# A trunk kernel on one core: weight rows spread by TensorE instead of by DMA, and three of eight channel blocks convolved by TensorE instead of two

## What is computed

```python
def rms_norm(x, g):
    xf = x.astype(jnp.float32)
    y = xf * lax.rsqrt(jnp.mean(xf * xf, axis=-1, keepdims=True) + NORM_EPS)
    return (y * g.astype(jnp.float32)).astype(x.dtype)
...
def conformer_conv(hn, w_in, b_in, w_dw, b_dw, ln_g, ln_b, w_out, b_out):
    a = hn @ w_in + b_in
    u, gate = jnp.split(a, 2, axis=-1)
    u = u * jax.nn.sigmoid(gate)
    u = lax.conv_general_dilated(u, w_dw[:, None, :], window_strides=(1,),
                                 padding=((CONV_WIDTH - 1, 0),),
                                 dimension_numbers=('NWC', 'WIO', 'NWC'),
                                 feature_group_count=D_MODEL) + b_dw
    u = jax.nn.silu(layer_norm(u, ln_g, ln_b))
    return u @ w_out + b_out
...
        q = (xc @ w_q).reshape(PEER_TOKEN_CHUNK, PEER_HEADS, 2, PEER_D_HALF)
        s = jnp.einsum('thcd,hcnd->thcn', q, subkeys, preferred_element_type=jnp.float32)
        s_top, i_top = lax.top_k(s, PEER_TOPK)
        cand = s_top[:, :, 0, :, None] + s_top[:, :, 1, None, :]
        cand_idx = i_top[:, :, 0, :, None] * PEER_N_KEYS + i_top[:, :, 1, None, :]
        best, pos = lax.top_k(cand.reshape(PEER_TOKEN_CHUNK, PEER_HEADS, PEER_TOPK * PEER_TOPK), PEER_TOPK)
        idx = jnp.take_along_axis(cand_idx.reshape(PEER_TOKEN_CHUNK, PEER_HEADS, PEER_TOPK * PEER_TOPK), pos, axis=-1)
        g = jax.nn.softmax(best, axis=-1)
        u = u_tab[idx]
        act = jax.nn.gelu(jnp.einsum('td,thkd->thk', xc, u), approximate=False)
        v = v_tab[idx]
        return jnp.einsum('thk,thkd->td', (g * act).astype(v_tab.dtype), v)
...
        h = h + mix
        h = h + peer_ffn(rms_norm(h, norm_ffn[layer]), peer_w_q[layer], peer_subkeys[layer],
                         peer_u[layer], peer_v[layer])
    return rms_norm(h, norm_final)
```

## Time and profile before

| | |
|---|---|
| median of 3 runs | 1570.3 us (1569.29 to 1572.05) |
| profiled execution, its own time | 1571.79 us |
| its span in the profile | 1570.0 us |
| busy: TensorE, its weight loads | 1026.8 us (65%), 505.7 us (32%) |
| busy: VectorE | 1100.7 us (70%) |
| busy: ScalarE, GpSimd | 597.5 us (38%), 602.9 us (38%) |
| moved by DMA | 613.86 MB, 391 GB/s over the span |
| mean granted clock of TensorE | 0.733 of 2.4 GHz |

### The profile page before, as it was taken

How to read it: one execution, slowest core, us unless ns; L and a number is a source line. 1 busy time by engine, 2 the same in 40 slices (tenths; PEclk the granted TensorE clock), 3 DMA queues, 4 the chain that set the end, 5 groups by cost and what they waited for, 6 DMA issues and landing times.

```text
span 1570.0 us, 20460 instructions
## 1 busy us (share of the span) xinstructions
PE 1026.8 (65%) x6572; PEld 505.7 (32%) x6572; DVE 1100.7 (70%) x2959; ACT 597.5 (38%) x1794; POOL 602.9 (38%) x516
## 2 busy tenths in 40 slices
PE   7988766667467677766676677467677645544443
PEld 3545422323234345322244355123234301101000
DVE  3433877776445679999665679699876676666764
ACT  2222455452143434444343434344434523332321
POOL 0002444443323345644334356244434444433441
PEclk9999996577777688667889799556688855555555
DMA  9627999999999999999999999999999999999996
GB/s 393 215 74 305 379 418 420 412 419 393 418 398 415 417 418 404 393 419 392 419 415 415 417 416 408 420 416 402 409 397 391 418 419 418 420 419 419 420 419 258
DMA packets 96156, 613.86 MB, mean 391 GB/s; under 512 B 11057, under 2 KB 16433, under 8 KB 27441
## 3 DMA queue, kind: packets, MB, share of 16 engines
q0 software_dynamic: 73728, 536.90, 83.3%
q1 hardware_dynamic: 21600, 75.47, 12.3%
q10 hardware_dynamic: 720, 0.18, 0.1%
HBM read 611.46 MB, written 1.05 MB: 390 GB/s over the span
## 4 chain that ended last, share of the span: by engine, by line
DMA 34%; DVE 27%; PE 19%; issue 12%; ACT 6%; POOL 2%; DVEq 0%; SPq 0%; POOLq 0%; ACTq 0%
DMA ring<-table_dram,idx 28%; DVE ring L1614 11%; PE bank L587 8%; PE ypsum L587 4%; DVE arena L1499 4%; PE qpsum L587 4%; DMA head<-heads_dram 3%; PE spsum L587 2%; POOL ring L580 2%; ACT L1030 2%; DMA arena<-c_out_dram 1%; ACT ring L1030 1%; DVE topi L1548 1%; ACT wts L1030 1%; PE bank L592 1%
## 5 line engine op out<-in xcount | busy, mean ns | idle before, releaser
L580 POOL DMA_INDIRECT ring<-table_dram,idx x512 | 602.7, 1177 | 942.3 <-PE ypsum L587 674.3
L1614 DVE CUSTOM_DVE_ANT_0 ring<-xns,ring 128x1024 f32<-128x1024 f32 x512 | 622.7, 1222 | 306.2 <-DMA ring<-table_dram,idx 303.1
L587 PE MATMUL ypsum<-ring,wts 128*32 128x256 f32 x4096 | 427.4, 512 | 453.8 <-ACT wts L1030 451.5
L1030 ACT ACTIVATE gel<-dot 128x1 f32<-128x1 f32 x512 | 103.3, 202 | 770.5 <-DVE dot L1614 769.1
L587 PEld LDWEIGHTS ypsum<-ring,wts 128*32 128x32 f32 x4096 | 100.1, 126 | 703.5 <-ACT wts L1030 654.4
L1030 ACT ACTIVATE wts<-gident,gel 128x32 f32<-128x32 f32 x512 | 164.6, 321 | 17.0 <-ACT gel L1030 0.2
L587 PE MATMUL qpsum<-head,hT 128*128 128x256 f32 (+1 forms) x308 | 92.8, 462 | 28.1 <-DMA head<-heads_dram 24.2
L1030 ACT ACT_TABLE_LOAD x84 | 107.8, 1283 | 8.5 <-PE bank L592 7.0
L1499 DVE SCALAR_TENSOR_TENSOR arena<-arena,cols 128x128 f32<-128x128 f32 x360 | 103.9, 344 | 0.7
L587 PEld LDWEIGHTS qpsum<-head,hT 128*128 128x128 f32 (+1 forms) x308 | 68.4, 230 | 50.9 <-issue 21.9
L587 PE MATMUL bank<-hT,arena 128*128 128x128 f32 x512 | 76.9, 312 | 2.8 <-issue 2.8
(11 more groups left out here) (162 smaller groups left out, 1045.5 us busy)
## 6 DMA issues: line engine op xcount, KB each, us to landing
head<-heads_dram SPq DMA_DIRECT2D x28, 512.0 KB, 9.2
ring<-w_in_dram SPq DMA_DIRECT2D x4, 2048.0 KB, 17.1
ring<-table_dram,idx POOLq DMA_INDIRECT x512, 12.6
arena<-c_in_dram SPq DMA_DIRECT2D x4, 2048.0 KB, 15.4
arena<-heads_dram SPq DMA_DIRECT2D x7, 1152.0 KB, 25.2
arena<-heads_dram SPq DMA_DIRECT2D x26, 256.0 KB, 5.1
arena<-c_out_dram SPq DMA_DIRECT2D x6, 1024.0 KB, 10.8
arena<-w_out_dram SPq DMA_DIRECT2D x1, 4096.0 KB, 38.5
```

What stands on the lines that cost most here:

```text
L580: pool.indirect_dma_start(out=row(b), out_offset=None, in_=table[:, :], in_offset=bass.IndirectOffsetOnAxis(ap=idx[R % 2][:, k:k + 1], axi ...
L587: return nc.tensor.matmul(o_, l, r, start=start, stop=stop, **kw)
L1030: return nc.scalar.activation(out_, in_, func, **kw)
L1614: V.tensor_tensor_reduce(out=u, in0=xnr[G % 2], in1=u, scale=1.0, scalar=0.0, op0=ALU.mult, op1=ALU.add, accum_out=dot[:, k:k + 1]).then_i ...
```

## The change

1. The norm weights of phases 1 to 3 and of the final norm, and the convolution's bias, are loaded as one row into partition 0 only. TensorE spreads the row over 128 partitions: a product of a row of ones (`ones`, 1x128) with the row (1x512) for each half. For a norm this takes two bank jobs more (`N_ROW`), filled by `gains` one slot before VectorE's norm (slot 93 or 94; slot 80 of the last phase), and VectorE reads the weights out of the banks in two instructions of 128x512 instead of one of 128x1024. For the bias the product is added to `conv_out`'s bank, and VectorE's addition of the bias and the wait behind it go. Phase 0's weights still come in the old way.
2. Block 5's taps go from VectorE to TensorE and ScalarE: TensorE makes blocks 6, 7 and 5, VectorE first 0, 1, 2, then 3 and 4. The slots over which they are spread stay. In VectorE's second part each tap waits for all but the last instruction instead of all but the last two.
3. Two small tiles move into the space of another (`posi`, `posf`), and the final norm signals each half.

```diff
-N_PROJ, N_NORM = 2 + len(PROJ_CHUNKS), 2
+N_PROJ, N_NORM = 2 + len(PROJ_CHUNKS), 4
+N_ROW = 2
...
-GLU_ORDER = [0, 1, 2, 6, 7, 3, 4, 5]
+GLU_ORDER = [0, 1, 2, 6, 7, 5, 3, 4]
...
-DVE_TAPS = [(c, k) for three in ((0, 1, 2), (3, 4, 5)) for k in range(TAPS) for c in three]
-PE_TAPS = [(c, k) for c in (6, 7) for k in range(TAPS)]
+DVE_TAPS = [(c, k) for some in ((0, 1, 2), (3, 4)) for k in range(TAPS) for c in some]
+PE_TAPS = [(c, k) for c in (6, 7, 5) for k in range(TAPS)]
...
             def load_gain(p):
                 n = min(p // TILES, LAYERS)
-                sp.dma_start(xn, gains_in[n:n + 1, :].to_broadcast([P, D])).then_inc(gain_in, 16)
+                if p == 0:
+                    sp.dma_start(xn, gains_in[n:n + 1, :].to_broadcast([P, D])).then_inc(gain_in, 16)
+                else:
+                    sp.dma_start(xn[0:1, :], gains_in[n:n + 1, :]).then_inc(gain_in, 16)
...
-                sp.dma_start(cbias, c_bout[0:1, :].to_broadcast([P, D])).then_inc(cbias_in, 16)
+                sp.dma_start(cbias[0:1, :], c_bout[0:1, :]).then_inc(cbias_in, 16)
...
-                last = gemm(CONV_AT[t] + J_CW + i, [hT_[:, k, :] for k in range(KD)], [cout[:, k, :] for k in range(KD)], CHUNK, half)
+                j, n = CONV_AT[t] + J_CW + i, out_half(t, i) * CHUNK
+                bank = bank_of(pe, j) if half == 0 else banks[bank_no(j)]
+                for k in range(half * KD // 2, (half + 1) * KD // 2):
+                    last = mm(bank[:, :], hT_[:, k, :], cout[:, k, :], k == 0, False)
                 if half == 0:
                     last.then_inc(cout_taken, 1)
+                else:
+                    pe.wait_ge(cbias_in, 16 * (t + 1))
+                    mm(bank[:, :], ones[0:1, :], cbias[0:1, n:n + CHUNK], False, True).then_inc(bank_full[bank_no(j)], 1)
...
+            def gains(p):
+
+                pe.wait_ge(gain_in, 16 * (p + 1))
+                for half in range(2):
+                    j = NORM_AT[p] + half
+                    bank = bank_of(pe, j)
+                    mm(bank[:, :], ones[0:1, :], xn[0:1, half * CHUNK:(half + 1) * CHUNK], True, True).then_inc(bank_full[bank_no(j)], 1)
...
+                if s == NORM_SLOT[p - 1] - 1:
+                    gains(p)
                 if s == NORM_SLOT[p - 1] + 1:
                     turn_input(p)
...
-                dve.wait_ge(cbias_in, 16 * (t + 1))
-                V.tensor_tensor(xs, xs, cbias[:, n:n + CHUNK], ALU.add).then_inc(half_done, 1)
-                dve.wait_ge(half_done, 2 * t + i + 1)
...
-                dve.wait_ge(gain_in, 16 * (p + 1))
-                V.scalar_tensor_tensor(out=xn, in0=xt(p % TILES), scalar=r, in1=xn, op0=ALU.mult, op1=ALU.mult)\
-                 .then_inc(xn_ready, 1)
+                for half in range(2 if p else 0):
+                    j, at_ = NORM_AT[p] + half, slice(half * CHUNK, (half + 1) * CHUNK)
+                    full(dve, j)
+                    free(j, V.scalar_tensor_tensor(out=xn[:, at_], in0=xt(p % TILES)[:, at_], scalar=r, in1=banks[bank_no(j)][:, :],
+                                                   op0=ALU.mult, op1=ALU.mult))
```

More of the change, by code:

```diff
@@ L85 @@
 NORM_AT += [CONV_AT[0] + N_CONV, CONV_AT[1] + N_CONV]
+NORM_AT.append(NORM_AT[PHASES - 1] + N_NORM)
 BANKS = 3
@@ L302, in build @@
         smalli = sb("smalli", 2, i32)
-        posi = sb("posi", TILES, i32)
-        posf = sb("posf", TILES)
+        posi, posf = sel[:, 0:TILES].bitcast(i32), sel[:, TILES:2 * TILES]
         rnorm = sb("rnorm", TILES)
         warm = sb("warm", 1)
+        ones = sb("ones", P)
         rows, rinv = part["sums"][:, 0:ATTN_HEADS], part["sums"][:, ATTN_HEADS:2 * ATTN_HEADS]
@@ L853, in beside_conv @@
                     conv_out(t, 1, s - 90)
-            def turn_input(p):
-                pe.wait_ge(xn_ready, p + 1)
-                turn_over(NORM_AT[p], xn)
+            def gains(p):
[4 more added lines that the diff above has]
+                    mm(bank[:, :], ones[0:1, :], xn[0:1, half * CHUNK:(half + 1) * CHUNK], True, True).then_inc(bank_full[bank_no(j)], 1)
+            def turn_input(p):
+                if p == 0:
+                    pe.wait_ge(xn_ready, 1)
+                else:
+                    for half in range(2):
+                        emptied(pe, NORM_AT[p] + half)
+                turn_over(NORM_AT[p] + N_ROW, xn)
             def replicate(G):
@@ L889, in head_queries @@
                 if p and h == 0:
-                    emptied(pe, NORM_AT[p])
-                    emptied(pe, NORM_AT[p] + 1)
+                    emptied(pe, NORM_AT[p] + 2)
+                    emptied(pe, NORM_AT[p] + 3)
                 bank = bank_of(pe, q_job(H))
@@ L995, in _ @@
             turn_input(0)
-            emptied(pe, NORM_AT[0])
-            emptied(pe, NORM_AT[0] + 1)
+            pe.wait_ge(ones_ready, 1)
+            emptied(pe, NORM_AT[0] + 2)
+            emptied(pe, NORM_AT[0] + 3)
             early_heads()
@@ L1023, in _ @@
                     beside_heads(p + 1, s)
+                elif s == FINAL_SLOT - 2:
+                    gains(PHASES)
         @block.scalar
@@ L1137, in take_taps @@
                 full(act, j)
-                for i in range(2):
+                for i in range(len(PE_TAPS) // TAPS):
                     c = PE_TAPS[i * TAPS][0]
@@ L1206, in turn_input @@
                 for i in range(2):
-                    take(NORM_AT[p] + i, xnT[:, 4 * i:4 * i + 4, :].rearrange("p k t -> p (k t)"))
+                    take(NORM_AT[p] + 2 + i, xnT[:, 4 * i:4 * i + 4, :].rearrange("p k t -> p (k t)"))
             def replicate(G):
@@ L1497, in tap @@
                     return
-                own.wait(2)
+                own.wait(2 if c < 3 else 1)
                 own.did(V.scalar_tensor_tensor(
@@ L1666, in final @@
                 r = rms(xt(t), D)
-                dve.wait_ge(gain_in, 16 * (PHASES + 1))
-                V.scalar_tensor_tensor(out=xt(t), in0=xt(t), scalar=r, in1=xn, op0=ALU.mult, op1=ALU.mult)\
-                 .then_inc(final_ready, 1)
+                for half in range(2):
+                    j, xs = NORM_AT[PHASES] + half, xt(t)[:, half * CHUNK:(half + 1) * CHUNK]
+                    full(dve, j)
+                    V.scalar_tensor_tensor(out=xs, in0=xs, scalar=r, in1=banks[bank_no(j)][:, :], op0=ALU.mult, op1=ALU.mult)\
+                     .then_inc(final_ready, 1)
             project(0)
             project(1)
+            V.memset(ones[:, :], 1.0).then_inc(ones_ready, 1)
             dve.wait_ge(ident_in, 2 * 16)
```

13 lines of the change are left out of this document (8 added, 5 removed).

## The result

The changed kernel took 1560.2 us (median of 6 runs, 1558.1 to 1562.6) against 1569.8 for the kernel before in the same session: a ratio of 0.9944, 95% interval 0.9932 to 0.9956, which is 8.8 us less (6.9 to 10.7); the two medians by themselves are 9.6 apart. That is inside the range, 3 us above the forecast. The profiled execution took 1561.3 us, its span 1559.4, 10.6 less than the one before; this is a difference of two single executions, and the ratio is the firmer number.

The account below looks back on a forecast made before the run. The prediction took DMA transfers at 419 GB/s as the bound. From a median of 1570.3 us, loads -7.5, taps -7.0 and ends +0.6, +0.5, +0.2 summed to -13.2, giving 1557.1 us, with a range of 1551 to 1566.

Parts of the forecast that it names:

- What bounds it: Whole kernel: DMA transfers are the limit, at a full rate of 419 GB/s; no gather slot can average under 2.50 us.
- The six loads: Four norm and two bias loads shrink from 128 rows to one, each saving 1.25 us at full rate: -7.5 us.
- the low bound: Four of the six loads lie in tap stretches where DMA is short of work; if worthless, only 2.5 us remain.
- The taps: In both tap stretches, 31 taps a convolution leave VectorE, regaining seven tenths of 9.9 us lost: -7.0 us, bounds 0 and 9.9.
- 412 GB/s or more: Sign of success: DMA's rate in the two tap stretches, before at 402 and 410 GB/s, reaches at least this.
- ScalarE and TensorE: In the tap stretches they take 31 more taps, 10.5 us on ScalarE and 13.3 on TensorE each, covered on average.
- 0.43 us a tap: TensorE's cost in the tap stretches for one more tap, at 1.2 GHz; 31 make 13.3 us.
- The ends: Convolution ends +0.6 us, later weights +0.5, final norm and the rest +0.2, where the row spreading adds work.
- the quarter counted for the weights' second half: Second output product's later weights, asked for 0.92 us later: a quarter counted, +0.5 us in all, bounds 0 and 1.8.
- A: Rival: only the bytes pay; TensorE's and ScalarE's lateness in the tap stretches replaces VectorE's; 1564.1 us, chance 0.18.
- B: Rival: not measurably faster; the taps bring nothing and loads inside the tap stretches only filled idle time; 1569.1 us, chance 0.07.
- C: Rival: slower, TensorE becomes the bound while taps run if its clock falls to about 1.2 GHz; 1580.6 us, chance 0.07.

Follow-up runs that it names:

- wide loads: The changed kernel with its six one-row loads made 128 rows wide again, TensorE's spreading kept: ratio 0.9981 to the kernel before, 3.0 us faster.
- taps only: The kernel before with block 5's taps moved from VectorE to TensorE and ScalarE, all loads unchanged: ratio 0.9988 to the kernel before, 1.9 us faster.
- taps off the routing slots: The changed kernel with VectorE's taps put only in slots where it has no routing, same work: ratio 0.9945 to the kernel before, 8.6 us faster.
- four blocks: The changed kernel with six diagonal buffers and a fourth block's taps (block 4) moved off VectorE: ratio 0.9930 to the kernel before, 11.0 us faster.
- queries first: The changed kernel with the head's queries ahead of the products spreading the next rows, in TensorE's order only: ratio 0.9941 to the kernel before, 9.3 us faster.
- six diagonals: The changed kernel with six diagonal buffers instead of four, so ScalarE may run further ahead: ratio 0.9943 to the kernel before, 8.9 us faster.

## Why the prediction came out as it did

**What bounds it.** Right. In all four pairs that differ by the 3.1 MB alone or by the rows and their spreading, the one that moved more was slower, and the last phase (1260 to 1540 us) moved 417 to 420 GB/s in every kernel of the table.

**The six loads, -7.5 us.** Right in this kernel, within the noise: 5.8 us between the changed kernel and its twin with wide loads, 6.9 beside taps only, 7.5 once the tap stretches are at full rate. The fear behind the low bound, that loads inside the stretches fill idle time, was real in part as well: with the old taps the six are worth 4.2, between the bounds of 2.5 and 7.5. The prediction's reason for the high end, that the next term removes what leaves DMA idle, points the right way: the same rows are worth more with the new taps.

**The taps, -7.0 us.** The mechanism was right, the size was not: this is the term that was mis-sized. It measured 1.9 us by itself and 4.6 on top of the rows, 3.5 by the windows. "So of the 9.9 us I take seven tenths" was a guess by the average: VectorE's 141 us under DMA's 145. The average came out as worked out (141.87), but much of the loss was made in the five routing slots of a round, where one tap in six fewer changes little: the wait before the gather shown fell from 4.1 to 3.4, under the 4 us that the prediction had named, but far from gone. The rate named as the sign, 412 GB/s or more, was not reached either: it was 410 and 411, in the second stretch hardly above the 410 before. Moving the taps out of those slots took it to 416 and 419 with no less work.

The second thing that the prediction lacked is that losses are not added. Taps only took 4.6 us of loss out of the stretches and gave 1.9 us of time, taps off the routing slots took out 5.3 us and gave none, and in the kernel before 6.2 and 1.9. An explanation: a gather that comes late in the stretch leaves DMA behind the engines, with more issued and not yet landed; a version that is ahead meets the convolution's end and the heads with a shorter queue and loses there. It fits the windows of the versions with the taps off the routing slots, and shortening one hold gave 3.6 us with full stretches (2.2 with four blocks) and 0.5 without them, differences of the size of the intervals. One window speaks against it: queries first alone lost 1.6 us at the convolution's end without full stretches (409 and 412 GB/s):

```profile
738.00:760.00 22.00, 18.29 (x77) 7.14 (x78) 14.47 (x35) 10.73 (x28) 8.83 (x8) 0.85 0.99 388
```

That the length of the queue is what carries it was argued from these, not measured by itself.

**ScalarE and TensorE.** 0.43 us a tap was too dear. The group `qpsum<-arena` went from 248 records and 72.2 us to 372 and 86.7: 14.5 us for 62 taps, 0.23 each, while the clock granted in the stretches rose from 0.73 and 0.65 to 0.77 and 0.70 of 2.4 GHz. Executions with equal work differ in it, but not so far: in the first stretch the three kernels with 62 taps on TensorE had 0.68 to 0.73, the eight with 93 had 0.75 to 0.82, the three with 124 had 0.83 to 0.86. More products ran, and a larger share of the stretch had the upper of the two levels (1.2 and 2.4 GHz). The Trainium skill, "TensorE: Matmul & The Clock Gate", section "What's actually happening", says that activity releases the throttle; the runs agree. TensorE was 72% busy in the first stretch, not the 120 us of 150 foreseen. ScalarE's new wait of 5.8 us wasn't foreseen and was covered, as six diagonals show.

**The ends, +1.3 us.** Not seen. VectorE's four waits before the addition behind the second product are 11.9 us in sum; they were 12.2. The later bank is made up by the bias addition that is gone, and the quarter counted for the weights' second half shows nowhere. The norm is 0.13 us longer, between the row's +0.10 and the +0.19 estimated from the Trainium skill, "VectorE: DVE Perf Modes", section "The TRN2 errata"; nothing in the time hangs on it. The sum was -13.2; with the taps at -3.5, the bytes at -7.4 and the ends at nothing it is -10.9, and the profiled spans give -10.6. The ratio gives -8.8 (6.9 to 10.7), so up to 2 us of this sum may be the chance of two executions. That the forecast lies only 3 us off is partly luck: the +1.3 that wasn't there made up for some of what the taps didn't bring.

**The rivals.** A, that only bytes pay, would have been 1564.1; the changed kernel is under it, and taps on the rows are worth 4.6 us, so it is out, although the truth lies halfway to it. B is out in this kernel; with the old taps, where it gave the rows 2.5 us, they are worth 4.2, so it holds in part. C is out by the run with four blocks, and its own condition, a clock near 1.2 GHz over the stretch, moved away as taps were added.

**What stays open.** The convolution's end, 346 to 374 GB/s for 22 us in the better versions: which of the waits there, VectorE's norm ahead of the dots or TensorE in the output product, sets it wasn't tried. The windows lie at fixed times while the versions run ahead of each other, so they show where DMA stood idle and don't add up to a time: the profiled execution of queries first alone took 1556.6 us, that with the taps off the routing slots besides 1559.2, against the order of their medians.

## What to carry to other kernels

Where DMA is the bound, bytes are worth their full time only as far as no engine sets the pace around them: find the stretches in which another engine is full, and relieve these in the same change. Read such an engine's load in the slots that produce what the next transfer waits for, not as the mean of the stretch; moving work out of those slots did more for the transfer rate here than taking work away. And expect part of a gain to be lost again at the next place where the engines hold buffers, as it was in three kernels here, perhaps because a stream that is on time meets that place with less in its queue: so look for the longest gap between issues before counting it.

## What the runs showed of the hardware

A product of one row with one row costs TensorE no less than a full one. The bias row onto 128x512 took 1.12 us for two records, of which eight full ones at the same clock took 3.70 (0.92 for two). The Trainium skill, "TensorE: Matmul & The Clock Gate", section "Why this matters for your kernels", says that a single product over 32 rows takes the same time as one over 128; the rows here, with one row, go the same way.

GpSimd's time to issue a gather is not constant. Over the 512 gathers of the changed kernel:

```profile
L586 POOL DMA_INDIRECT ring<-table_dram,idx x512: 935/942/2020, 126.2 to 1533.7; - x171
```

The minimum and median are 0.94 us and the maximum is 2.02; in the kernel before, the gather of 638.19 took 2.01 with a dot (638.17) and taps on VectorE beside it. What makes one long was not isolated.
